# Eight experts fed from one sorted gather instead of one gather each, and their scatter moved to the turn between two experts

## The chip, the core and the metric

One core of a Trainium2 chip runs the whole kernel as one program. The metric is the device time in microseconds (us) of one execution. The core has five engines with their own instruction streams: PE (TensorE, matmuls), DVE (VectorE), ACT (ScalarE), POOL (GpSimd) and SP (SyncE, which here only issues DMAs). They meet at semaphores. SBUF holds tiles of 128 partitions; PE writes into eight PSUM banks of 128 x 512 float32.

## The reference

Two layers of a decoder trunk over 256 tokens of width 1024. Each has a token mixer and then a feed-forward part: a dense SwiGLU in layer 0, and in layer 1 eight SwiGLU experts of hidden width 3584, of which each token uses the best two. What matters here is the second:

```
def _moe(h, router_w, router_b, wg, wu, wd):
    logits = (h @ router_w + router_b).astype(jnp.float32)
    top_v, top_i = lax.top_k(logits, MOE_TOPK)
    top_w = jax.nn.softmax(top_v, axis=-1)
    gates = jnp.sum(top_w[..., None] * jax.nn.one_hot(top_i, N_EXPERTS, dtype=jnp.float32), axis=-2)
    out = jnp.zeros_like(h)
    for e in range(N_EXPERTS):
        out = out + gates[..., e:e + 1] * _swiglu(h, wg[e], wu[e], wd[e])
    return out
```

The result is added to x through a per-channel gate, and a last RMSNorm follows. 256 tokens with two picks each make 512 (token, expert) pairs, spread unevenly over the experts.

## The kernel before

Everything is float32. About half of the time goes to the mixers and the dense part, which the change leaves alone. The expert part begins with the router, at 1033 us, and runs to the end.

**Weights.** An expert is 42 units of 1 MB: seven groups `g`, each with two gate units, two up units and two down units. SP streams them through 14 slots (L485); a slot is loaded again when PE has used its unit, so SP follows PE by at most 14 units. The first 14 units of the first expert are loaded before the router is done.

**Router (L1740 to L1776).** DVE picks the two best experts of each token as masks. PE turns the masks into running counts, five products of 8 columns each (L941 to L945). A token's count within an expert, less one, is its key. DVE compares the keys with a row of slot numbers, `slot_f`, and this gives `p_m`, the gather matrix of one expert (L1774). Expert 0 comes first and the other seven follow in an order worked out on the chip from their counts, by turns a crowded and a light one; `ranks`, `places`, `counts`, `turns`, `gates`, `keys` and `expert_gates` are small steps of DVE for this, put between the copies of the first gather.

**Gather (L955, L981).** For each expert, eight column blocks m: two products (two token tiles) of `h_tm` with `p_m` into one of the banks 6 and 7, then a DVE copy to `xg` (L1835, L1854). It writes 256 slots where the expert has over 128 tokens, else 128. It stands between two experts in the program of PE (the block `tail` of `expert_loop`), and the next expert's first product waits for the copies.

**Expert body.** There are six variants by the rounded token count n: 32 (`quarter_rows`), 64, 96, 128 (`rows_stationary`), 160 and 256 (`weights_stationary`). Its sums for the output lie in banks 2 to 5, and ACT takes them out to `ysb` at the end (L1440, L1275).

**Scatter (L966 to L978).** The output of expert e is put back to its tokens while expert e+1 runs: after groups 1 to 4 of the next expert, one step each, into banks 6 and 7, where DVE adds it to `xT` (L1846). Each step waits for the merges of the step before. At the end of the last expert the four steps stand alone. The scatter matrix `pgT` is made in two moves: DVE compares keys, times gates, into `pg_m` (`matrices`), and before the last down product PE transposes it (`prepare`, L1185) and DVE copies it (L1949). In the first expert the scatter steps run on a zero matrix.

The branches on counts (`by_rows`, `by_size`, the compare chain of L450 and L453) are executed by each engine's own sequencer.

Of the kernel before, what the change touches and what calls it, by code (L numbers as in the profile page):

```python
# [17 lines left out]
P = 128  # L18
# [75 lines left out]
def trunk(nc, x_cols, c_cols, par_cols, ada_units, dense_units, moe_units, out):  # L94
# [7 lines left out]
    with ctx:  # L102
# [30 lines left out]
        stk = sb("stk", [P, QUARTER])  # L133
        modc = sb("modc", [P, 48])
# [7 lines left out]
        key9 = sb("key9", [P, TT, EXPERTS + 1])  # L142
        gate9 = sb("gate9", [P, TT, EXPERTS + 1])
# [28 lines left out]
        xg = proj[:, 16:24, :]  # L172
        h_tm = proj[:, 24:32, :].rearrange("p (t a) n -> p t (a n)", t=TT)
        p_m = proj[:, 32:34, :]
        pg_m = proj[:, 34:36, :]
        pgT = proj[:, 36:38, :]
        silx = proj[:, 38:42, :].rearrange("p (b j) n -> p b (j n)", b=2)
        hst = proj[:, 42:46, :].rearrange("p (b j) n -> p b (j n)", b=2)
        o_tm = proj[:, 24:32, :].rearrange("p (t a) n -> p t (a n)", t=TT)
# [34 lines left out]
        order_c = swap[:, 192:256].rearrange("p (a b) -> p a b", a=8)  # L214
        gr = xc[:, 0:6, :].rearrange("p (a b) n -> p a b n", a=3)
# [104 lines left out]
        p_s = sem("gather_matrix")  # L320
        pg_s = sem("scatter_matrix")
# [99 lines left out]
        def expert_loop(eng, expert, between=None):  # L421
# [13 lines left out]
            if between is not None:  # L435
                with nc.body(tail, valid_engines=own):
# [8 lines left out]
                    between(following, coming)  # L445
                    eng.br(head)
            with nc.body(head, valid_engines=own):
                e = nc.snap(index, engines=own, min_val=0, max_val=EXPERTS - 1)
                count, before = on(now), on(past)
                to_form[SIZES[-1]] = eng.br_cond(count > SIZES[-2], f"{tag}_{SIZES[-1]}", f"{tag}_over_{SIZES[-3]}")  # L450
# [6 lines left out]
            for n in SIZES:  # L457
                with nc.body(f"{tag}_{n}", valid_engines=own):
                    ahead = eng.mark_branch_hint_location()
                    after = expert(n, e, before)  # L460
# [129 lines left out]
        def _(pe):  # L590
# [350 lines left out]
            mm(ps[:, 1, 0:8], striu[:, :], mask[:, 0, :], start=True, stop=True)  # L941
            mm(ps[:, 1, 8:16], ones[:, :], mask[:, 0, :], start=True, stop=False)
            mm(ps[:, 1, 8:16], striu[:, :], mask[:, 1, :], start=False, stop=True)
            mm(ps[:, 1, 16:24], ones[:, :], mask[:, 0, :], start=True, stop=False)
            mm(ps[:, 1, 16:24], ones[:, :], mask[:, 1, :], start=False, stop=True).then_inc(cum_s, 1)  # L945

            C_BASE, PER = KT, 1 + 2 * KT

            def gather(free_at, n):  # L950

                for m in range(KT):
                    pe.wait_ge(cf_s, free_at + m)
                    for t in range(TT):
                        last = mm(ps[:, 6 + (m + 1) % 2, 0:n], h_tm[:, t, m * P:(m + 1) * P], p_m[:, t, 0:n],  # L955
                                  start=(t == 0), stop=(t == TT - 1))
                    last.then_inc(c_s, 1)

            pe.wait_ge(htm_s, TT)
            pe.wait_ge(p_s, 1)  # L960
            gather(CF0 + C_BASE - 1, SEQ)
            pe.wait_ge(rk_s, 2)
            C1 = C_BASE + KT

            def scatter(n, step, free_at):

                pe.wait_ge(cf_s, free_at + 2 * step)
                for c in range(2):
                    m = step + 4 * c
                    if n == HALF:  # L970
                        r0 = HALF * c
                        mm(ps[:, 6 + c, 0:SEQ], ysb[r0:r0 + HALF, 0, step * P:(step + 1) * P], pgT[r0:r0 + HALF, 0, :],
                           start=True, stop=True).then_inc(c_s, 1)
                        continue
                    for st in range(n // P):
                        last = mm(ps[:, 6 + c, 0:SEQ], ysb[:, st, m * P:(m + 1) * P], pgT[:, st, :],
                                  start=(st == 0), stop=(st == n // P - 1))
                    last.then_inc(c_s, 1)  # L978

            def gather_next(following, count):  # L980
                pe.wait_ge(p_s, following + 1)  # L981
                with pe.If(count <= P):
                    gather(following * PER + CF0 + C1 + KT - PER, P)
                with pe.Else():
                    gather(following * PER + CF0 + C1 + KT - PER, SEQ)

            def expert(n, e, before):
# [7 lines left out]

                def tokens_ready(kind, g, h):
                    if kind == "g" and g == 0:
                        pe.wait_ge(cf_s, e * PER + CF0 + C1 - 4 * (1 - h))

                def rows_stationary(n):  # L1000
# [67 lines left out]
                def quarter_rows(n):  # L1068
# [44 lines left out]
                    for g in range(1, GE):  # L1113
                        gate(g)
                        sum_and_turn(g - 1)
# [3 lines left out]
                        if 1 <= g <= 4:  # L1119
                            scatter_before(g - 1)  # L1120
                        down_quarter(g - 1)
                    sum_and_turn(GE - 1)
                    prepare(n)
# [4 lines left out]
                def weights_stationary(n):  # L1128
# [30 lines left out]
                    for g in range(GE):  # L1159
# [4 lines left out]
                        if 1 <= g <= 4:  # L1164
                            scatter_before(g - 1)
                        if g:
                            down_wide(g - 1)
                    prepare(n)
# [3 lines left out]

                def scatter_before(step):

# [22 lines left out]
            def scatter_last(rows):  # L1197
                for step in range(4):
                    scatter(rows, step, PER * EXPERTS + CF0 + C1 - KT)

# [856 lines left out]
```

## Time and profile before

| | |
|---|---|
| median of three runs | 2001.78 us (2000.38 to 2004.81) |
| the profiled execution | 2002.5 us, its span 2000.6 us |
| PE busy | 1872.0 us (94%) |
| DVE, ACT, POOL busy | 509.1, 279.6, 351.7 us |
| DMA | 533.87 MB, mean 267 GB/s |
| expert part, first product to the end of the last down product | 1055.5 to 1973.6 us |

The experts in their order, from PE's timeline:

| place | n | first product | last product ends |
|---|---|---|---|
| 0 | 32 | 1055.5 | 1133.2 |
| 1 | 160 | 1140.3 | 1330.6 |
| 2 | 32 | 1336.3 | 1411.9 |
| 3 | 128 | 1419.1 | 1571.0 |
| 4 | 32 | 1575.9 | 1652.5 |
| 5 | 96 | 1658.5 | 1783.6 |
| 6 | 64 | 1791.0 | 1872.7 |
| 7 | 64 | 1877.9 | 1973.6 |

PE's busy share of 94% says little by itself: where PE waits for weights, a shorter program of PE ends no earlier. So the views by stretch and the timeline of PE are what to read: which stretch ends with a wait for DMA, and which doesn't.

### The profile page before, as it was taken

The numbers are of one execution on the slowest core, as the hardware profiler recorded it, in microseconds if no ns is written. First come the engines' busy times: TensorE is split into PE (matmuls) and PEld (weight loads), VectorE is DVE, ScalarE is ACT, GpSimd is POOL, SyncE is SP. The second block draws the span as 40 slices with busy tenths as digits, with TensorE's granted clock in tenths as the row PEclk, the third lists the DMA queues.
The fourth block names the chain that finished last, engine by engine and source line by source line (L and its number), as shares of the span: only waits on it lengthen the run. The fifth ranks groups of instructions, "written<-read, shape, count | busy, mean of one in ns | idle before, by whom it ended". The sixth has DMA issues, their size and how long they took to land.

```text
span 2000.6 us, 27713 instructions
## 1 busy us (share of the span) xinstructions
PE 1872.0 (94%) x11005; PEld 1313.5 (66%) x11006; DVE 509.1 (25%) x1131; ACT 279.6 (14%) x517; POOL 351.7 (18%) x215
## 2 busy tenths in 40 slices
PE   7999799989999899999978899998999989999986
PEld 5888588877777688888863587753444436555543
DVE  1794734110000285333332100011100110101111
ACT  2204212010000311423021000010000100010002
POOL 2709910059996000000000000000000000000000
PEclk8999899999999999999989899998999989999998
DMA  9645533157765344333458976669998899999994
GB/s 388 252 152 209 194 127 119 64 227 263 269 250 189 147 148 147 126 106 106 168 231 354 420 319 253 253 265 421 420 389 293 329 421 419 420 371 422 422 422 180
DMA packets 73845, 533.87 MB, mean 267 GB/s; under 512 B 8320, under 2 KB 8320, under 8 KB 8960
## 3 DMA queue, kind: packets, MB, share of 16 engines
q1 hardware_dynamic: 67680, 489.72, 62.2%
q0 software_dynamic: 5760, 41.95, 5.7%
q8 instruction: 92, 1.51, 0.3%
q10 hardware_dynamic: 288, 0.50, 0.1%
q14 instruction: 25, 0.20, 0.0%
HBM read 531.08 MB, written 1.05 MB: 266 GB/s over the span
## 4 chain that ended last, share of the span: by engine, by line
PE 81%; DMA 7%; SPq 4%; DVE 4%; ACT 2%; issue 2%; POOL 1%; ACTq 0%; DVEq 0%
PE ps L657 21%; PE ps L1012 12%; PE ps L720 8%; PE ps L729 7%; PE ps L1139 6%; PE ps L1047 6%; SPq L485 4%; PE ps L740 4%; PE ps L1155 3%; DMA ring<-in_moe_units 3%; PE ps L1075 3%; PE ps L955 2%; DMA sq<-in_moe_units 1%; DMA xc<-in_moe_units 1%; PE ps L1105 1%
## 5 line engine op out<-in xcount | busy, mean ns | idle before, releaser
L657 PE MATMUL ps<-hT,ring 128*128 128x256 f32 x2048 | 454.3, 383 | 5.0 <-ACT hT L1262 5.0
L657 PEld LDWEIGHTS ps<-hT,ring 128*128 128x128 f32 x2048 | 389.8, 192 | 61.9 <-issue 8.3
L576 POOL TENSOR_TENSOR aring<-aring,ccol 128x2048 f32<-128x2048 f32 x40 | 145.0, 3625 | 236.3 <-ACT hT L1262 162.6
L729 PE MATMUL ps<-hT,ring 128*128 128x256 f32 x704 | 156.7, 384 | 4.0 <-ACT hT L1262 4.0
L582 POOL TENSOR_TENSOR aring<-aring 128x1024 f32<-128x1024 f32 x80 | 149.5, 1869 | 6.3
L729 PEld LDWEIGHTS ps<-hT,ring 128*128 128x128 f32 x704 | 135.0, 193 | 22.8 <-issue 4.4
L1012 PE MATMUL ps<-ring,proj 128*64 128x256 f32 (+2 forms) x1144 | 131.6, 362 | 3.6 <-DMA ring<-in_moe_units 3.6
L1886 DVE TENSOR_TENSOR proj<-proj,ps 128x256 f32<-128x256 f32 (+2 forms) x28 | 14.6, 521 | 379.8 <-PE ps L1012 379.8
L1012 PEld LDWEIGHTS ps<-ring,proj 128*64 128x64 f32 (+2 forms) x1144 | 74.8, 132 | 55.3 <-issue 33.0
L1616 DVE SCALAR_TENSOR_TENSOR misc<-cpad,par,misc 128x256 f32<-128x256 f32 x240 | 102.7, 505 | 0.0
L1267 ACT ACTIVATE proj<-ps 128x512 f32<-128x512 f32 x64 | 38.2, 596 | 328.8 <-PE ps L657 328.8
L720 PE MATMUL ps<-proj,ring 128*128 128x256 f32 x384 | 83.4, 379 | 0.0
L720 PEld LDWEIGHTS ps<-proj,ring 128*128 128x128 f32 x384 | 72.8, 190 | 9.9
L740 PE MATMUL ps<-ring,proj 128*128 128x512 f32 x176 | 77.3, 592 | 0.0
L1385 ACT ACTIVATE proj<-ps 128x256 f32<-128x256 f32 (+2 forms) x28 | 13.0, 464 | 381.4 <-PE ps L1012 381.4
L1729 DVE TENSOR_TENSOR proj<-proj,ps 128x256 f32<-128x256 f32 x22 | 9.3, 421 | 210.8 <-ACT proj L1365 210.8
L1139 PE MATMUL ps<-proj,ring 128*128 128x160 f32 x416 | 60.0, 300 | 0.0
L720 PE MATMUL ps<-hT,ring 128*128 128x256 f32 x256 | 55.8, 380 | 3.0 <-DVE hT L1693 3.0
L1139 PEld LDWEIGHTS ps<-proj,ring 128*128 128x128 f32 x416 | 57.5, 190 | 0.8 <-issue 0.8
L740 PEld LDWEIGHTS ps<-ring,proj 128*128 128x128 f32 x176 | 33.4, 190 | 37.3 <-issue 36.8
L1094 PEld LDWEIGHTS ps<-stk,proj 128*128 128x128 f32 x336 | 44.3, 212 | 20.1 <-issue 20.1
L720 PEld LDWEIGHTS ps<-hT,ring 128*128 128x128 f32 x256 | 48.5, 190 | 10.3 <-DVE hT L1693 3.8
(347 smaller groups left out, 2086.2 us busy)
## 6 DMA issues: line engine op xcount, KB each, us to landing
ring<-in_moe_units SPq DMA_DIRECT2D x144, 1024.0 KB, 17.0
ring<-in_dense_units SPq DMA_DIRECT2D x121, 1024.0 KB, 5.0
aring<-in_moe_units SPq DMA_DIRECT2D x48, 1024.0 KB, 17.3
proj<-in_moe_units SPq DMA_DIRECT2D x48, 1024.0 KB, 18.7
aring<-in_ada_units POOLq DMA_DIRECT2D x40, 1024.0 KB, 6.2
extra<-in_moe_units SPq DMA_DIRECT2D x24, 1024.0 KB, 16.6
xc<-in_moe_units SPq DMA_DIRECT2D x24, 1024.0 KB, 20.6
misc<-in_moe_units SPq DMA_DIRECT2D x24, 1024.0 KB, 19.7
```

The costliest lines, as they stand in the source:

```text
L485: sp.dma_start(eslot[u % EXP_SLOTS], moe_units[ds(expert, 1), u].rearrange("e p n -> p (e n)")).then_inc(efull[u % EXP_SLOTS], 16)
L576: last = g.tensor_tensor(w, w, ccol[:, :].unsqueeze(2).broadcast_to([P, KT, 256]), ALU.mult)
L582: last = g.tensor_tensor(dst, w[:, 0:half_k, :], w[:, half_k:2 * half_k, :], ALU.add)
L657: last = mm(ps[:, n % 2, j * SEQ:(j + 1) * SEQ], wide(s)[:, k, j * P:(j + 1) * P], hT[:, k, :], start=(k == 0), stop=(k == KT - 1))
L720: last = mm(ps[:, idx % 2, j * SEQ:(j + 1) * SEQ], view(s)[:, k, (cols + j) * P:(cols + j + 1) * P], rhs[:, k, :], start=(k == 0), stop=(k ...
L729: last = mm(ps[:, j, c0:c0 + n], wide(w)[:, k, j * P:(j + 1) * P], x_src[:, k, 0:n], start=(k == 0), stop=(k == KT - 1))
L740: last = mm(dst, hm[:, b, j, t * P:t * P + rows], rows2(slot)[:, j, hf * 512:(hf + 1) * 512], start=(first and j == 0), stop=(stop and j = ...
L1012: last = mm(ps[rows * c:rows * (c + 1), bank, 4 * t0:4 * (t0 + rows)], xg[:, 4 * h + k, t0:t0 + rows], w[:, k, 4 * rows * c:4 * rows * (c ...
L1047: last = mm(dst, hmt[:, g % 2, h0:h0 + rows], w[:, i, cols], start=(g == 0 and j == 0), stop=(g == GE - 1 and j == 3))
L1075: last = mm(ps[n * k:n * (k + 1), bank, :], xg[:, 4 * h + k, 0:n], w[:, k, :], start=(h == 0), stop=(h == 1))
L1139: last = mm(ps[:, j % 2, c0:c0 + n], w[:, k, j * P:(j + 1) * P], xg[:, 4 * h + k, 0:n], start=(h == 0 and k == 0), stop=(h == 1 and k == 3))
L1616: v.scalar_tensor_tensor(cacc[:, m, :], cpad[:, m, ds(k, SEQ)], cwcol[:, l, ds(k * CT + m, 1)], cacc[:, m, :], ALU.mult, ALU.add).then_inc ...
```

## The change

It replaces eight gathers by one, builds the scatter matrix another way, and moves the scatter.

1. **Gather.** Five running sums become eleven products of 8 columns: a token's slot now counts all pairs of lower experts too, so the 512 pairs have 512 sorted slots. `p_all` (two tiles of 128 x 512) holds both picks. One gather of eight column blocks by 512 columns fills `xg_all`; ACT copies the first 256 columns to `xg` for expert 0. For each later expert DVE copies its window of columns from `xg_all` to `xg`, 64, 128 or 256 wide, from a start read from `first_slot`, once its own work for the expert before is done.
2. **Scatter matrix.** PE spreads each token's slot numbers and gates along rows (eight products of 128 columns, after the gather); ACT takes them to `slot_rows` and `gate_rows`. In group 2 of an expert DVE compares `slot_rows` with the slot number of each row (`slot_of_row`) and multiplies by `gate_rows`. That is `pgT` itself: the transposes of `prepare` and their copy go.
3. **Scatter.** It moves out of the next expert's groups to the block between the experts, all four steps in one go, into the four banks 4 to 7. PE waits there for `pgT`, for the merges before, and for ACT's copy of the output (`ye_s`). The next expert's first product stands behind it in PE's queue. The dummy scatter in the first expert goes. The merges of DVE run after the scatter, while the next expert starts.

```
@@ PE, router
-            mm(ps[:, 1, 0:8], striu[:, :], mask[:, 0, :], start=True, stop=True)
...
+            lower = [(ones, below[:, t, :]) for t in range(TT)]
+            token_sums(0, lower + [(striu, mask[:, 0, :])])
+            token_sums(8, lower + [(ones, mask[:, 0, :]), (striu, mask[:, 1, :])])
+            token_sums(16, lower)
+            token_sums(24, [(ones, mask[:, t, :]) for t in range(TT)]).then_inc(cum_s, 1)
@@ PE, gather
-            gather(CF0 + C_BASE - 1, SEQ)
+            for m in range(KT):
+                if m >= 2:
+                    pe.wait_ge(cf_s, CF0 + KT + m - 1)
+                for t in range(TT):
+                    pe.wait_ge(p_s, t + 1)
+                    last = mm(ps[:, 6 + m % 2, :], h_tm[:, t, m * P:(m + 1) * P], p_all[:, t, :],
+                              start=(t == 0), stop=(t == TT - 1))
+                last.then_inc(c_s, 1)
+            for values, bank in ((token_slot, 3), (token_gate, 2)):
+                if bank == 2:
+                    pe.wait_ge(gate1_s, 1)
+                for pick in range(2):
                     for t in range(TT):
+                        c0 = (TT * pick + t) * P
+                        last = mm(ps[:, bank, c0:c0 + P], values[:, pick, t:t + 1].broadcast_to([P, P]), ident[:, :],
+                                  start=True, stop=True)
+                last.then_inc(row_s, 1)
@@ PE, between two experts (before: gather_next)
+            def scatter(n):
+                for step in range(4):
+                    for c in range(2):
+                        m = step + 4 * c
+                        dst = ps[:, 4 + 2 * (step // 2) + c, (step % 2) * SEQ:(step % 2 + 1) * SEQ]
...
+            def scatter_done(following, coming, done):
+                pe.wait_ge(pg_s, 2 * following)
+                pe.wait_ge(cf_s, following * PER + CF0 + C1 - PER)
+                pe.wait_ge(ye_s, following + 1)
+                by_rows(pe, done, scatter)
@@ PE, in each variant of the expert body
                         gate(g)
+                        if g == 1:
+                            banks_merged()
                         h_transpose(g - 1)
                         up(g)
-                        if 1 <= g <= 4:
-                            scatter_before(g - 1)
                         down_rows(g - 1)
                     h_transpose(GE - 1)
-                    prepare(n)
                     down_rows(GE - 1)
@@ ACT, before the experts
+            for m in range(KT):
+                act.wait_ge(cf_s, CF0 + KT + m + 1)
+                a_(xg[:, m, :], xg_all[:, m, 0:SEQ], ACT.Copy).then_inc(xg_s, 1)
+            for i, (rows, bank) in enumerate(((slot_rows, 3), (gate_rows, 2))):
+                act.wait_ge(row_s, i + 1)
+                a_(rows, ps[:, bank, :].rearrange("p (a b) -> p a b", a=2), ACT.Copy).then_inc(rows_s, 1)
@@ DVE, router
-            for t in range(TT):
-                last = v.tensor_scalar(p_m[:, t, :], slot_f[:, :], key9[:, t, 0:1], None, ALU.is_equal)
+            for t in range(TT):
+                last = v.tensor_scalar(p_all[:, t, :], slots, token_slot[:, 0, t:t + 1], None, ALU.is_equal)
+            then_wait(last)
+            for t in range(TT):
+                v.scalar_tensor_tensor(p_all[:, t, :], slots, token_slot[:, 1, t:t + 1], p_all[:, t, :],
+                                       ALU.is_equal, ALU.add).then_inc(p_s, 1)
...
-                v.tensor_copy(xg[:, m, :], ps[:, 6 + (m + 1) % 2, 0:SEQ]).then_inc(cf_s, 1)
+                v.tensor_copy(xg_all[:, m, 0:2 * SEQ], ps[:, 6 + m % 2, :]).then_inc(cf_s, 1)
@@ DVE, between two experts
+            def merged_next(following, coming, done):
                 def tokens(width):
+                    first = dve.value_load(first_slot[0:1, ds(following, 1)], min_val=0, max_val=5 * P - width)
+                    v.tensor_copy(xg[:, :, 0:width], xg_all[:, :, ds(first, width)]).then_inc(xg_s, KT)
+                by_rows(dve, coming, tokens)
+                for step in range(4):
+                    merge(step, following * PER + (C1 - PER))
@@ DVE, group 2 of an expert (before: matrices)
+                def matrix():
...
+                        v.scalar_tensor_tensor(picks, slot_rows, slot_of_row[:, kind + st, ds(e, 1)], gate_rows,
+                                               ALU.is_equal, ALU.mult).then_inc(pk_s, 1)
+                        v.tensor_tensor(pgT[:, st, :], picks[:, 0, :], picks[:, 1, :], ALU.add).then_inc(pg_s, 1)
```

## Rows read from the trace of the kernel before

**Rows 1.** Stretches: PE, PEld, DVE, ACT, POOL busy (count), granted clock, DMA share, GB/s

```profile
1150.00:1300.00 150.00, 150.00 (x997) 120.22 (x996) 11.71 (x35) 6.99 (x23) 0.00 (x0) 1.00 0.70 276
1345.00:1380.00 35.00, 33.05 (x252) 15.87 (x248) 8.54 (x19) 2.62 (x6) 0.00 (x0) 1.00 1.01 422
1780.00:1795.00 15.00, 12.04 (x110) 7.74 (x104) 2.34 (x8) 4.23 (x8) 0.00 (x0) 1.00 0.72 269
```

**Rows 2.** Chain of waits, router: start, us on the chain, what

```profile
1040.95 0.43 PE ps L942 x2
1042.66 1.56 issue
```

**Rows 3.** Timeline, router to first product: start, us, engine, line, what, count, [idle before]

```profile
1043.51 0.62 DVE L1774 TENSOR_SCALAR proj<-slot_f,key 128x256 f32<-128x256 f32 x2
1044.23 8.26 PE L955 MATMUL ps<-proj 128*128 128x256 f32 x28 [1.56 <-issue]
1055.53 1.92 PE L1075 MATMUL ps<-aring,proj 128*32 128x512 f32 x16 [1.42 <-DVE proj L1835]
```

**Rows 4.** Stretch at the start of the first gather

```profile
1044.00:1046.00 2.00, 1.77 (x4) 1.51 (x5) 0.61 (x2) 1.03 (x1) 0.00 (x0) 0.50 0.03 12
```

**Rows 5.** Timeline of PE: eight products of 512 columns in expert 3

```profile
1426.06 3.60 PE L1012 MATMUL ps<-extra,proj 128*128 128x512 f32 x8
```

**Rows 6.** Timeline of PE: last and first products around each turn between experts

```profile
1131.35 1.87 PE L1105 MATMUL ps<-sq,proj 128*32 128x512 f32 x8
1140.26 2.44 PE L1139 MATMUL ps<-proj,aring 128*128 128x160 f32 x16
...
1325.89 4.70 PE L1155 MATMUL ps<-sq,proj 128*128 128x512 f32 x24
1336.28 1.92 PE L1075 MATMUL ps<-aring,proj 128*32 128x512 f32 x16 [0.76 <-DVE proj L1854]
...
1410.83 1.04 PE L1105 MATMUL ps<-sq,proj 128*32 128x512 f32 x8
1419.09 7.13 PE L1012 MATMUL ps<-aring,proj 128*128 128x512 f32 x16 [1.43 <-issue]
...
1567.38 3.60 PE L1047 MATMUL ps<-sq,proj 128*128 128x512 f32 x8
1575.92 1.92 PE L1075 MATMUL ps<-aring,proj 128*32 128x512 f32 x16 [0.76 <-DVE proj L1854]
...
1651.13 1.40 PE L1105 MATMUL ps<-sq,proj 128*32 128x512 f32 x8
1652.83 4.44 PE L955 MATMUL ps<-proj 128*128 128x128 f32 x32 [0.29 <-issue]
1658.50 4.47 PE L1012 MATMUL ps<-aring,proj 128*64 128x256 f32 x56 [1.23 <-DVE proj L1854]
...
1780.68 2.94 PE L1047 MATMUL ps<-sq,proj 128*64 128x512 f32 x24
1791.02 3.67 PE L1012 MATMUL ps<-aring,proj 128*64 128x256 f32 x32 [1.74 <-issue]
```

**Rows 7.** Timeline of ACT: the output taken out, n = 160 and 64

```profile
1330.65 2.50 ACT L1275 ACTIVATE proj<-ps 128x512 f32<-128x512 f32 x6 [18.37 <-PE ps L1155]
1973.61 0.60 ACT L1440 ACTIVATE proj<-ps 128x512 f32<-128x512 f32 x1 [4.15 <-PE ps L1047]
```

**Rows 8.** Timeline of PE: one scatter step, for 32 or 64, 96 or 128, and 160 rows

```profile
1202.71 0.70 PE L972 MATMUL ps<-proj 64*128 64x256 f32 x4
...
1345.32 1.99 PE L976 MATMUL ps<-proj 128*128 128x256 f32 x8
...
1584.96 1.13 PE L976 MATMUL ps<-proj 128*128 128x256 f32 x4
```

**Rows 9.** Timeline of PE: the last scatter and the sums of the last norm

```profile
1976.68 1.23 PE L972 MATMUL ps<-proj 64*128 64x256 f32 x4 [3.12 <-issue]
...
1984.39 4.68 PE L635 MATMUL ps<-sq,ones 128*128 128x256 f32 x16
```

More of the change, by code:

```diff
@@ L448, in expert_loop @@
                 e = nc.snap(index, engines=own, min_val=0, max_val=EXPERTS - 1)
-                count, before = on(now), on(past)
+                count = on(now)
                 to_form[SIZES[-1]] = eng.br_cond(count > SIZES[-2], f"{tag}_{SIZES[-1]}", f"{tag}_over_{SIZES[-3]}")
@@ L459, in expert_loop @@
                     ahead = eng.mark_branch_hint_location()
-                    after = expert(n, e, before)
+                    after = expert(n, e)
                     nc.regs_mov(past, count)
@@ L962, in _ @@
[L962 to L987, printed above, removed]
+            below = rt[:, 13, :, :]
+            def token_sums(c0, terms):
+                for i, (weights, values) in enumerate(terms):
+                    last = mm(ps[:, 1, c0:c0 + EXPERTS], weights[:, :], values, start=(i == 0), stop=(i == len(terms) - 1))
+                return last
@@ L1171, in weights_stationary @@
                     return after
-                def scatter_before(step):
-                    pe.wait_ge(ye_s, e + 1)
-                    by_rows(pe, before, lambda rows: scatter(rows, step, e * PER + CF0 + C1))
-                def prepare(n):
-                    slot_tiles = (n + P - 1) // P
-                    pe.wait_ge(pg_s, e + 1)
-                    pe.wait_ge(cf_s, e * PER + CF0 + C1 + KT)
-                    for st in range(slot_tiles):
-                        for t in range(TT):
-                            last = nc.tensor.transpose(ps[:, 6, st * SEQ + t * P:st * SEQ + (t + 1) * P],
-                                                       pg_m[:, t, st * P:(st + 1) * P], ident[:, :])
-                    last.then_inc(c_s, 1)
                 if n == QUARTER:
@@ L1191, in expert @@
                 return rows_stationary(n) if n <= P else weights_stationary(n)
-            expert_loop(pe, expert, gather_next)
+            expert_loop(pe, expert, scatter_done)
             last_count = pe.value_load(cnt[0:1, EXPERTS:EXPERTS + 1], min_val=0, max_val=SEQ)
-            pe.wait_ge(ye_s, EXPERTS + 1)
-            def scatter_last(rows):
-                for step in range(4):
-                    scatter(rows, step, PER * EXPERTS + CF0 + C1 - KT)
-            by_rows(pe, last_count, scatter_last)
+            scatter_done(EXPERTS, None, last_count)
             norm_sums(2 * DEPTH)
@@ L1745, in _ @@
             narrow_copy(DEPTH)
+            v.memset(xg_all[:, :, 2 * SEQ:], 0.0)
+            v.tensor_copy(slots[:, 0:SEQ], slot_f[:, :])
+            v.tensor_scalar(slots[:, SEQ:2 * SEQ], slot_f[:, :], float(SEQ), None, ALU.add)
             dve.wait_ge(lg_s, 1)
```

205 lines of the change are left out of this document (101 added, 104 removed).

## The prediction

> **What bounds the kernel now.** I read the stretches first, then PE's timeline around each turn between two experts, then the chain of waits in the router. The change touches nothing before the router, so only the time from 1040 us on is in play.
>
> The stretches show two kinds of expert [rows 1]. In place 1 (n = 160) PE is busy all the time at full clock and the DMA engines at a share of 0.70: PE bounds, and each microsecond off its program counts. In place 2 (n = 32) DMA is full and PE has gaps: the weights bound. By the same reading places 0, 2, 4 and 7 are of the second kind, places 1, 3 and 5 of the first. The third stretch is the turn from place 5 to 6: DMA is idle for 28% of 15 us, 4.2 us, because all 14 slots are full and SP waits for PE to use a unit. After that turn places 6 and 7 need 70 more units, and the stream is full to the end, so the end of place 7 is set by when place 6 begins.
>
> From this follows how a saving is passed on. In a weight-bound expert the stream restarts when the expert's first units are used, because before the turn the slots are full. An edit inside it is worth nothing, an edit that moves its first product moves its end by as much. In a PE-bound expert both count. In places 6 and 7 nothing inside counts, the turn between them neither. What counts is therefore: the router up to the first product of place 0; the six turns 0 to 1 up to 5 to 6; the program of places 1, 3 and 5; and what follows the last down product.
>
> **Router.** The running sums take 0.43 us a product on the chain [rows 2]. Eleven instead of five: +2.6. Three small compares more for the masks, without waits, 0.3 (0 to 0.6). From the last sum to the gather's first product it was 1.56 us [rows 2], in which two compares of 256 columns took 0.62 [rows 3]. Now: two small steps (0.4), two compares of 512 columns (1.24, twice the row), one compare-and-add of 512 (0.75 by the same row, 0.6 to 1.0) and a semaphore, 2.5: +0.9. Together +3.8.
>
> From the gather's first product to the first expert product it was 11.3 us [rows 3]: the gather waited for copies. The new gather has 8 x 2 products, in float32 two passes each, 32 instructions of 512 columns. One costs 0.43 to 0.45 at full clock [rows 5], so 13.8 us. DVE has 1.7 us for each block, and its copy and small step need about 1.4, so PE sets the pace. The granted clock was 0.50 at the start of the gather, which is 1.2 GHz [rows 4]; PE had been nearly idle before it. I keep about 3.5 us at the half clock, +1.7 (0 to 2.5). Then come the eight row products, 16 instructions of 128 columns; 32 such take 4.44 [rows 6], so 2.2. They stand ahead of expert 0 in PE's program and nothing hides them; ACT's copies to `xg` are done meanwhile. Last the count is loaded and the compare chain run: 1.42 before [rows 3], and I take 1.7 as the sequencer can hardly do it sooner. Sum 19.4, so +8.1. The router costs **+11.9** (8.5 to 16).
>
> **The six turns.** The time between the end of the last down product and the next expert's first product was [rows 6]: 7.0, 5.7, 7.2, 4.9, 6.0 and 7.4 us, mostly gather. The new turn has four parts. (a) ACT takes the output out: 0.6 for n = 32 or 64, 2.5 for n = 160 [rows 7]; n = 96 needs six copies too, n = 128 two, 1.1; plus 0.1 to start. (b) After this wait the sequencer branches on the count and issues. No row shows a branch behind a wait inside the loop. From below: the old gather began 0.29 after the last product [rows 6]. From above: the last scatter began 3.12 after it [rows 9], 2.4 of it after ACT's copy. I take 0.4, since the turns inside the loop run the same block as the old gather while the last scatter first leaves the loop. (c) Four scatter steps. A step costs 0.63 to 0.70 for up to 64 rows, 1.06 for 96 or 128, 1.93 for 160 [rows 8]: 2.5, 4.25 or 7.7. (d) The jump into the next expert. It left PE idle for 0.76 to 1.74 [rows 6]. A long scatter hides it. Behind a short one I put 0.5, 2.5 and 1.3 at turns 0, 2 and 4, more where the old row says "issue" with 1.43.
>
> New turns: 4.1, 10.7, 6.1, 5.9, 4.9, 7.3. Differences: -2.9, +5.0, -1.1, +1.0, -1.1, -0.1, together +0.8. The second is the telling one: the scatter of 160 rows costs nothing today, in the middle of weight-bound place 2, and 7.7 us in the open afterwards. Two turns idle PE for about 3 us, and after a gap of 3.12 the last scatter ran at half rate (1.23 for a step that takes 0.70 otherwise [rows 8, 9]), so +1.3. Turns: **+2.1** (-3 to +14).
>
> Queued behind PE's new wait for ACT is the whole next expert, and behind that SP, which loads only as units are used. DVE's copy of the window to `xg` lies beside the last down products and the merges beside the next expert's first products: 0.
>
> **Inside places 1, 3 and 5.** Four scatter steps go from each, 12 at 0.70 [rows 8]: -8.4. `prepare` goes too. In places 3 and 5 its transposes lie in a wait for ACT, 0; in place 1 four of them at 0.14 are on the path, -0.5. The new comparison of rows on DVE is hidden, DVE being busy for 12 of 150 us there [rows 1]. **-8.9** (-9.5 to -8).
>
> **The end.** Today the four last steps wait for merges in turn, and from the first step to the end of the norm's sums it is 12.4 us [rows 9]. With four banks: 4 x 1.18 plus 4.68, 9.4. **-3.0** (-4.5 to -2).
>
> **Sum.** +11.9 +2.1 -8.9 -3.0 = +2.1. On the profiled execution's 2002.5 that is 2004.6; this execution lies 0.7 above the median, so **2003.9** for the median. A measurement of this kernel can tell about 0.2% (4.0 us) from no change: faster means below 1997.8, slower above 2005.8.
>
> **Rivals.**
>
> (1) *Faster: the clock and the jumps.* If PE has risen to full clock before the gather (the longer sums keep it busier) 1.7 goes; if the gaps at the turns don't drop it, 1.3; if the jumps are hidden behind short scatters too, 3; and a shorter start of place 0, 0.6. Together -6.6: 1997.3. For it: 2.4 and 1.3 are small gaps next to the 7 us that preceded the half clock in the router. Against: the clock was down after 3.12 us at the end [rows 9]. It decides from about 6.1 us of such gains. Chance 0.18.
>
> (2) *Slower: the branch behind the wait.* Each turn pays 2.4 after ACT's copy [rows 7, 9] instead of 0.4, six times 2.0: 2015.9. Against: the old tail has branches too and starts its gather within 0.29 at best [rows 6]. Chance 0.12. The Trainium skill speaks for this rival and so against this change: "Runtime: NRT & Kernel Launch", section "Instruction fetch mechanics", says that prefetch is sequential, and that a taken branch to a target outside the pages at hand stalls until a DMA has fetched it. The new block between experts is longer than the old one, and its branch comes after a wait. By that rule the sum would be this rival's; by the 0.29 us the forecast's.
>
> (3) *Slower: the gather follows its copies.* The copy to `xg_all` is twice as wide, and DVE's small steps lie between; if a block takes 2.2 us instead of 1.7, +4: 2007.9. Chance 0.12.
>
> (4) *The saving inside the experts is not there.* Between places 4 and 6 I save 4.0 us, and DMA has 4.2 of idle time to give [rows 1]; if it has less, because units of 2.5 us come in at the wrong moment, or if a crowded expert begins before its first four units are there, 1 to 2 us are lost: 2005.4. Chance 0.08.
>
> **Numbers.** The forecast itself has 0.50, with 1999.5 to 2008.5 as its own range. Of it 0.33 is within 0.2%, 0.13 slower, 0.04 faster. Rival 1 gives 0.10 faster, 0.08 same; rival 2 0.12 slower; rival 3 0.10 slower, 0.02 same; rival 4 0.03 slower, 0.05 same. Faster 0.14, same 0.48, slower 0.38. The range runs from 1997.5 to 2011.5; it leaves rival 2 out and the far half of rival 1.
>
> **What the profile after would show.** First product of place 0 near 1067.4. Six turns of the lengths above, that of the 160-row scatter near 11 us with 7.7 of PE work. Places 1, 3 and 5 shorter by 3.3, 2.8 and 2.8 from first to last product; places 0, 2 and 4 as long as before, with more idle time of PE. Two pairs of merges after the last scatter and no wait between its steps. The prediction fails if the gather's blocks lie more than 1.9 us apart, if scatters begin more than 1 us after ACT's copy, or if places 0, 2 and 4 change their length by more than 1.5 us: then the weight stream is not what I think.

## The result

Before and after ran four times each. Every kernel of an experiment below has its ratio to the kernel before as it ran on the same chip in the same session.

| | median (lowest to highest) us | profiled execution: time, span | granted clock |
|---|---|---|---|
| before | 2001.08 (1999.86 to 2004.81) | 2002.5, 2000.6 | 0.967 |
| after | 2016.18 (2014.7 to 2017.57) | 2014.96, 2013.2 | 0.955 |

The ratio is 1.0069, 95% interval 1.0055 to 1.0083: 0.69% slower. The forecast was 2003.9 with a range of 1997.5 to 2011.5, so both missed. The time is that of rival 2 (2015.9). Whether its mechanism is the cause as well is the first question.

The page of after (engines' busy us, share of the span, instructions; then shares of the chain that ended last):

```profile
PE 1861.8 (92%) x10775; PEld 1302.4 (65%) x10776; DVE 492.8 (24%) x1066; ACT 283.7 (14%) x527; POOL 351.3 (17%) x215
PE 78%; DMA 8%; SPq 6%; DVE 3%; issue 2%; ACT 2%; POOL 1%; ACTq 0%; DVEq 0%
```

The router, in PE's timeline of after (start, us, line, what, count, [idle before]; compare rows 2 and 3):

```profile
1038.23 0.61 PE L958 MATMUL ps<-heads,ones 128*128 128x8 f32 x4 [1.66 <-DVE heads L1780]
...
1044.16 16.80 PE L976 MATMUL ps<-proj 128*128 128x512 f32 x32 [2.30 <-DVE proj L1793]
1060.79 1.05 PE L985 MATMUL ps<-ident,token_slot 128*128 128x128 f32 x8
1061.68 1.06 PE L985 MATMUL ps<-ident,token_gate 128*128 128x128 f32 x8
1062.67 1.92 PE L1102 MATMUL ps<-aring,hT 128*32 128x512 f32 x15
```

Its clock at the start of the gather (start:end, length, busy times, granted clock, DMA share, GB/s):

```profile
1044.00:1048.00 4.00, 3.84 (x5) 1.81 (x6) 1.09 (x7) 0.00 (x0) 0.00 (x0) 0.50 0.00 0
1048.00:1052.00 4.00, 4.00 (x8) 1.67 (x8) 2.22 (x8) 0.83 (x2) 0.00 (x0) 0.77 0.00 0
```

The gather's 32 instructions take 16.8 us, those of the first 4 us at the half clock, and no wait for a copy splits the row. The first expert product stands at 1062.67 instead of 1055.53. The work ahead of the router, which the change doesn't touch, ran 2.4 us ahead of that in the trace of before. So the change costs 9.5 here.

The turns of after, from the same view (compare rows 6 and 8; a turn is the stretch between two experts, and turn 0 stands behind place 0):

```profile
1140.06 2.00 PE L998 MATMUL ps<-proj 64*128 64x256 f32 x16 [1.67 <-ACT proj L1449]
1146.41 4.63 PE L1165 MATMUL ps<-hT,aring 128*128 128x160 f32 x16 [4.36 <-issue]
...
1339.02 8.86 PE L1002 MATMUL ps<-proj 128*128 128x256 f32 x32 [3.14 <-ACT proj L1277]
1347.81 1.07 PE L1102 MATMUL ps<-aring,hT 128*32 128x512 f32 x8
...
1426.41 2.00 PE L998 MATMUL ps<-proj 64*128 64x256 f32 x16 [0.86 <-ACT proj L1449]
1432.93 10.12 PE L1040 MATMUL ps<-aring,hT 128*128 128x512 f32 x16 [4.52 <-issue]
```

Two things are to be seen. The scatter follows ACT's copy closely: at turn 2 it begins 0.86 us after the last product, and 0.6 of that is the copy (at turn 0 it is 1.67). But behind a short scatter PE stands for 4.4 and 4.5 us on "issue" before the next expert's first product, where the forecast had 0.5 and 2.5. And the next expert's first 16 instructions then take 4.63 and 10.12 us, which took 2.44 and 7.13 before [rows 6]: the half clock follows the gap. The stretch behind turn 0 says the same (columns as above):

```profile
1146.00:1150.00 4.00, 3.59 (x13) 3.60 (x14) 0.00 (x0) 0.00 (x0) 0.00 (x0) 0.50 1.02 418
1150.00:1154.00 4.00, 4.00 (x23) 4.00 (x23) 0.00 (x0) 0.09 (x1) 0.00 (x0) 0.72 1.00 416
```

The end (compare rows 9) has one wait, then all steps, then the sums. From the last down product's end (1991.08) to the end of the sums it takes 10.5 us instead of 15.5.

```profile
1994.28 2.79 PE L998 MATMUL ps<-proj 64*128 64x256 f32 x16 [3.20 <-issue]
1997.07 4.54 PE L648 MATMUL ps<-sq,ones 128*128 128x256 f32 x16
```

The same reading of PE's timeline gives this table. Besides before and after it has five kernels of the experiments below. A place's length goes from its first product to the end of its last down product, a turn from there to the next first product (us). The last column is the stretch from the first product of place 6 to the end of place 7.

| kernel | first product | places 0 to 5 | turns 0 to 5 | 6 and 7 |
|---|---|---|---|---|
| before | 1055.5 | 77.7 190.3 75.6 151.9 76.6 125.1 | 7.0 5.7 7.2 4.9 6.0 7.4 | 182.6 |
| after | 1062.7 | 75.7 189.5 77.7 151.6 79.6 122.9 | 8.0 11.9 7.4 5.2 7.5 8.6 | 182.8 |
| code shifted (r_align) | 1062.2 | 78.2 188.3 77.7 148.6 75.6 122.9 | 5.4 11.9 5.0 5.2 6.9 8.6 | 182.6 |
| before, shifted badly (r_cross) | 1054.3 | 80.3 192.9 79.6 153.7 75.7 126.5 | 13.4 5.7 10.1 4.9 11.3 8.4 | 182.3 |
| filled turn (r_late) | 1065.5 | 79.8 186.5 79.6 148.5 75.5 121.3 | 18.8 24.1 16.7 19.0 17.0 20.7 | 182.0 |
| early hints (r_inline2) | 1063.8 | 78.0 187.1 77.3 148.6 76.9 122.0 | 2.7 9.8 2.7 4.9 4.5 9.4 | 182.3 |
| and scatter in groups (r_groups2) | 1061.9 | 77.4 192.8 76.4 151.9 79.2 124.5 | 1.2 0.9 1.5 0 0 0.7 | 191.1 |

### The profile page after: what moved, and what is told of

Read it like the earlier page. It is cut to its first block, busy times and chain, and to the rows that moved or that the text cites. A ratio compares the mean times of both kernels' runs of the same rounds, so it can differ in the third digit from the quotient of the medians.

```text
span 2013.2 us, 26982 instructions
## 1 busy us (share of the span) xinstructions
PE 1861.8 (92%) x10775; PEld 1302.4 (65%) x10776; DVE 492.8 (24%) x1066; ACT 283.7 (14%) x527; POOL 351.3 (17%) x215
## 4 chain that ended last, share of the span: by engine, by line
PE 78%; DMA 8%; SPq 6%; DVE 3%; issue 2%; ACT 2%; POOL 1%; ACTq 0%; DVEq 0%
PE ps L670 21%; PE ps L1040 11%; PE ps L733 8%; PE ps L742 7%; PE ps L1165 6%; SPq L498 6%; PE ps L1075 5%; PE ps L753 4%; PE ps L1181 3%; DMA sq<-in_moe_units 3%; PE ps L1102 2%; DMA ring<-in_moe_units 1%; DMA xc<-in_moe_units 1%; DMA misc<-in_ada_units 1%; PE ps L1121 1%
## 5 line engine op out<-in xcount | busy, mean ns | idle before, releaser
L670 PEld LDWEIGHTS ps<-hT,ring 128*128 128x128 f32 x2048 | 390.7, 192 | 62.2 <-issue 8.3
L742 PEld LDWEIGHTS ps<-hT,ring 128*128 128x128 f32 x704 | 136.6, 195 | 23.5 <-issue 4.4
L595 POOL TENSOR_TENSOR aring<-aring 128x1024 f32<-128x1024 f32 x80 | 148.5, 1857 | 6.3
L1040 PE MATMUL ps<-ring,hT 128*64 128x256 f32 (+2 forms) x1144 | 132.3, 362 | 5.4 <-DMA ring<-in_moe_units 5.4
L1040 PEld LDWEIGHTS ps<-ring,hT 128*64 128x64 f32 (+2 forms) x1144 | 75.4, 132 | 57.2 <-issue 34.3
L733 PEld LDWEIGHTS ps<-proj,ring 128*128 128x128 f32 x384 | 72.8, 190 | 9.9
L753 PE MATMUL ps<-ring,proj 128*128 128x512 f32 x176 | 77.3, 592 | 0.0
L1121 PEld LDWEIGHTS ps<-stk,proj 128*128 128x128 f32 x336 | 48.6, 230 | 21.9 <-issue 21.9
L1165 PE MATMUL ps<-hT,ring 128*128 128x160 f32 x416 | 60.0, 300 | 0.0
L1165 PEld LDWEIGHTS ps<-hT,ring 128*128 128x128 f32 x416 | 57.5, 190 | 0.8 <-issue 0.8
L1102 PE MATMUL ps<-ring,hT 128*32 128x512 f32 x312 | 46.0, 692 | 10.9 <-DMA ring<-in_moe_units 10.9
## 6 DMA issues: line engine op xcount, KB each, us to landing
ring<-in_moe_units SPq DMA_DIRECT2D x144, 1024.0 KB, 15.6
proj<-in_moe_units SPq DMA_DIRECT2D x48, 1024.0 KB, 18.8
extra<-in_moe_units SPq DMA_DIRECT2D x24, 1024.0 KB, 15.4
```

The lines of the kernel that those rows point to most:

```text
L595: last = g.tensor_tensor(dst, w[:, 0:half_k, :], w[:, half_k:2 * half_k, :], ALU.add)
L670: last = mm(ps[:, n % 2, j * SEQ:(j + 1) * SEQ], wide(s)[:, k, j * P:(j + 1) * P], hT[:, k, :], start=(k == 0), stop=(k == KT - 1))
L733: last = mm(ps[:, idx % 2, j * SEQ:(j + 1) * SEQ], view(s)[:, k, (cols + j) * P:(cols + j + 1) * P], rhs[:, k, :], start=(k == 0), stop=(k ...
L742: last = mm(ps[:, j, c0:c0 + n], wide(w)[:, k, j * P:(j + 1) * P], x_src[:, k, 0:n], start=(k == 0), stop=(k == KT - 1))
L753: last = mm(dst, hm[:, b, j, t * P:t * P + rows], rows2(slot)[:, j, hf * 512:(hf + 1) * 512], start=(first and j == 0), stop=(stop and j = ...
L1040: last = mm(ps[rows * c:rows * (c + 1), bank, 4 * t0:4 * (t0 + rows)], xg[:, 4 * h + k, t0:t0 + rows], w[:, k, 4 * rows * c:4 * rows * (c ...
```

## The experiments

**What the leap waits for.** A form is the code for one rounded token count. First thing in the tail, the block between two experts, PE's program gives a hint which form comes next (`mark_branch_hint_location`). Behind the tail's work it branches there; this far branch is the leap. The trace has records of PE's sequencer and of the DMA packets that bring its code. One such packet has 16384 bytes, a piece of code; in the compiled program that is 256 instructions of 64 bytes. Read from these records, in us:

```
turn  kernel  hint     far branch, took  code packet      hint to branch's end
 0    before  1131.90  1139.42  0.43     1135.7           7.9
 2    before  1412.40  1417.63  1.13     1416.2           6.4
 4    before  1652.00  1657.35  0.74     1655.6           6.1
 0    after   1139.19  1140.73  5.33     1143.6           6.9
 2    after   1424.09  1427.23  5.28     1430.0           8.4
 4    after   1667.07  1671.15  5.30     1674.0           9.4
```

The first kernel shifts the code of after:

```diff
+            if unused is not None:            # in expert_loop, ahead of the tail
+                with nc.body(f"{tag}_unused", valid_engines=own):
+                    unused()                  # 45 matmuls, reached by no execution
+                    eng.br(end)
```

> The changed kernel with 45 matmuls added that are never executed: they stand in TensorE's program ahead of the end-of-expert code and shift its addresses, so that the scatter, the hint and the far branch of an expert's end lie in one 16 KB piece of code instead of across two. Nothing that runs is changed. Theory A (fetching the next piece of code while the scatter runs throws away what the hint has fetched, and the leap into the next expert waits for a whole fetch): after turns 0, 2 and 4 the idle time ahead of the next expert's first instruction falls from 4.4, 4.5 and 2.9 us by 2 to 3.5 each, turn 5's scatter ends sooner, and the half-clock products after it go; 2004 to 2008 us. Theory B (the hint comes too shortly ahead of the branch, 1.5 to 4.1 us, or the branch overtakes it; where the code lies is of no account): no change, 2015 to 2017 us.

Measured: 2003.95 us, ratio to before 1.0007 (0.9997 to 1.0016). Nothing that is executed differs from after, and 12.2 us of median are gone (12.4 by the two ratios). Its turns 0 and 2:

```profile
1141.25 2.00 PE L1002 MATMUL ps<-proj 64*128 64x256 f32 x16 [0.86 <-ACT proj L1457]
1145.79 3.47 PE L1169 MATMUL ps<-hT,aring 128*128 128x160 f32 x16 [2.54 <-issue]
...
1424.57 2.00 PE L1002 MATMUL ps<-proj 64*128 64x256 f32 x16 [0.86 <-ACT proj L1457]
1428.75 7.13 PE L1044 MATMUL ps<-aring,hT 128*128 128x512 f32 x16 [2.19 <-issue]
```

The idle time is 2.5 and 2.2 instead of 4.4 and 4.5, and behind the shorter gap at turn 2 the first products run at full clock (granted 1.00, and 7.13 us). The place of the code was the cause of most of it, then, but not of the whole: the far branches of turns 0, 2 and 4 still take 3.6, 3.2 and 4.5 us. They end 6.4, 6.2 and 6.3 us after the hint, as at turns 2 and 4 of before. So with an undisturbed fetch the target is ready about 6.3 us after the hint, and the scatter of up to 64 rows leaves only 1.8 to 3.1 us between hint and branch (theory B's part).

The second kernel does the same harm to the kernel before. 13 such matmuls shift its tail across the same boundary:

> The kernel before with 13 matmuls added that are never executed, which shift the code of the gather between two experts so that it lies across two 16 KB pieces of TensorE's program. Nothing that runs is changed. Theory A (fetching the next piece throws away what the hint has fetched): the leap into the next expert, 0.4 to 1.2 us before, takes some 5 us at turns 0, 2, 4 and 5; with the clock's loss behind it 8 to 16 us more, 2009 to 2017. Theory B (only hint to branch time counts, which stays at 5 us and more here): no change, 2000 to 2003 us.

Measured: 2026.99 us, ratio 1.0115 (1.0098 to 1.0131), more than either theory said.

```profile
1134.54 8.04 PE L959 MATMUL ps<-proj 128*128 128x256 f32 x32
1148.04 4.63 PE L1143 MATMUL ps<-proj,aring 128*128 128x160 f32 x16 [5.47 <-issue]
...
1436.46 3.78 PE L1016 MATMUL ps<-aring,proj 128*128 128x512 f32 x4 [5.66 <-issue]
```

The far branches of turns 0, 2 and 4 take 6.1, 5.2 and 5.4 us. The six turns grow by 15.6 us in sum and the places 0 to 5 by 11.5 (table), partly at the half clock behind the gaps; why place 2, which follows no long gap, is 4.0 longer I can't say. Theory A's direction stands in both kernels. B is refuted as the sole cause, since here the hint comes 5.3 us and more ahead of the far branch. The packets come 12.3, 9.2 and 8.1 us after the hint, with none in between. So no fetched code was thrown away, as the expectation had it: the fetch started late.

The third fills the turn of after:

```diff
                 by_rows(pe, done, scatter)
+                if coming is not None:
+                    for _ in range(32):
+                        mm(ps[:, 0, 0:SEQ], ident[:, :], pgT[:, 0, :], start=True, stop=True)
```

> The changed kernel with 32 matmuls of 256 columns (about 3.4 us at full clock) executed behind the scatter of each of the six turns inside the loop, ahead of the branch into the next expert; their result is used by nobody. Theory B (the branch comes too soon behind the hint): the leap at turns 0, 2 and 4 falls from 5.3 to about 1 us, so those turns get some 1 us shorter each, and the turns 1, 3 and 5 3.4 longer: about +7, 2021 to 2025 us. Theory A (the hint is thrown away by the fetch of the next piece of code, and the tail still lies across two): the leap stays 5.3 us and all six turns get 3.4 longer: about +18 to +21 us, 2033 to 2037.

Measured: 2082.1 us, ratio 1.0391 (1.0368 to 1.0414). I had mis-sized the filling by four: a float32 product makes two instructions of 0.22 us each, so the filling takes 14 us a turn and the time says nothing about either theory. The trace does.

```profile
1149.87 14.39 PE L1013 MATMUL ps<-proj,ident 128*128 128x256 f32 x64
1164.09 2.20 PE L1168 MATMUL ps<-hT,aring 128*128 128x160 f32 x15
```

The leap is free (the branch takes 0.34), although the tail still lies across two pieces. So the hint isn't lost: it is held back. Its packet starts 6.1, 6.4 and 4.6 us after the hint, and each time 3.5 to 3.7 after the branch that leaves the scatter over the boundary (1146.23, 1455.20, 1715.17). The far branch comes only 9 to 11 us after the packet, so it can't have asked for it. In after, the same distance holds: the branch over the boundary stands at 1140.12, 1426.48 and 1670.27, and the packets come 3.5, 3.6 and 3.7 later. There, and at turns 2 and 4 of the second kernel, the packet also comes 2.7 to 2.9 us after the far branch, so these turns alone could not tell a held hint from a fetch that the branch began. Turn 0 of the second kernel, where the gather's last products cross the boundary without a branch, is the odd one: about 4 us from the crossing, 3.6 from the far branch.

The mechanism that fits these turns is an inference from their times: the fetch of the hinted piece starts only when TensorE's sequencer has left the first of the two pieces, and about 6 us from there on the target is ready. The Trainium skill ("Runtime: NRT & Kernel Launch", section "Instruction fetch mechanics") says that a sequencer holds two lines of 16 KiB, fetched in order, and that a taken branch outside them stalls for a DMA fetch. The traces agree: such a branch took 5.2 to 6.1 us here. With two lines, a third piece has to wait until one is left, as the held packets do. The same section also gives PE 128 KiB, more than two lines; the traces fit two.

**Taking the leap out.** In the next kernel PE's loop has no shared tail. Each form's own code ends with its scatter, whose size is known there, so the branch on the row count goes; the chain of compares follows. The hint is given earlier, ahead of the last two down products. Unused matmuls place the code so that no boundary comes late between hint and leap.

```diff
+                        if g == GE - 1:
+                            hint(after)          # ahead of the last two down products
                         down_rows(g - 1)
...
-            expert_loop(pe, expert, scatter_done)
+            scatter_loop(pe, expert, scatter_after, {32: 21, 96: 34, 128: 22})
```

> The changed kernel with TensorE's expert loop rearranged: the scatter of each form stands at the end of that form's own code (no shared tail, no branch on the row count), the hint for the next expert's form is given before the last two down products (9 us or so ahead of the leap instead of 1.5 to 4), and unused matmuls place the stretch from hint to leap within one 16 KB piece of code, or let the boundary come soon after the hint. Same products and scatters in the same order. Theory A (a leap is free when its code has been fetched, and the fetch is complete some 6.2 us after the hint, as in the shifted kernel): leaps of 0.3 to 1 us in all turns, so 8 to 9 us less at the turns than the shifted kernel, and one or two more from the clock: 1992 to 1997 us, faster than before. Rival (the leap costs its 3 to 4.5 us whatever the lead, or TensorE's gap is needed by another engine): 2002 to 2005 us.

Measured: 2004.08 us, ratio 1.0012 (1.0003 to 1.0022), which looks like the expectation's rival. Its trace shows something else, my own slip: the unused matmuls ahead of one form were executed once, behind the last expert.

```profile
1972.20 2.00 PE L1052 MATMUL ps<-proj 64*128 64x256 f32 x16 [0.79 <-ACT proj L1507]
1974.13 11.83 PE L465 MATMUL ps<-heads,ones 128*128 128x8 f32 x68
1985.89 1.65 PE L702 MATMUL ps<-sq,ones 128*128 128x256 f32 x3
```

With them truly out of the way:

> The kernel with early hints and scatters at the turn again, with the 34 unused matmuls now where they are never executed (in its first form they ran once behind the last expert and took 11.8 us of TensorE, seen in its trace). Nothing else changes. Theory A: 2004.1 less 11.8, or 1991 to 1994 us. Rival (the matmuls were hidden by the merges and squares that the norm sums wait for): 1997 to 2004.

Measured: 1993.86 us, ratio 0.9953 (0.994 to 0.9966): theory A.

```profile
1142.58 2.00 PE L1052 MATMUL ps<-proj 64*128 64x256 f32 x16 [0.81 <-ACT proj L1507]
1144.51 2.44 PE L1223 MATMUL ps<-hT,aring 128*128 128x160 f32 x16
```

No idle time stands ahead of the next expert and its first products take 2.44, as before. The turns 0 to 5 now sum to 34.0 us (after 48.6, before 38.2). The scatter begins 0.81 after the last down product, with no branch behind the wait for ACT. With that branch it was 0.86 (first kernel). So the branch, rival 2's mechanism, costs 0.05.

**Where the scatter belongs.** The same loop, but with part three of the change undone: the scatter is done in four steps of two banks within groups 1 to 4 of the next expert, each merged there.

```diff
+                        if 1 <= g <= 4:
+                            scatter_before(g - 1)
                         down_rows(g - 1)
...
-                    scatter_after(n, e)
```

> The same loop with early hints, but the third part of the change is undone: each expert's scatter is again done in four steps of two banks inside the groups 1 to 4 of the next expert (merged there by VectorE), the last one behind the loop; the gather into sorted slots and the new scatter matrix stay. Theory P (the scatter costs TensorE what it takes wherever it stands, and the last one in four banks saves the 5 us found at the end): about 3 to 8 us slower than the early-hint loop with scatters at the turn, 1996 to 2004 us. Rival (at the turn the scatter is dearer, because it waits for ScalarE's copy and idles TensorE into the slow clock, while inside the groups it has no wait): 3 to 8 us faster than that loop, below 1992 us.

Measured: 1994.11 us, ratio 0.9958 (0.9944 to 0.9972). That lies between the two theories, and level with the early-hint kernel. But this kernel has the old end, 15.4 us behind the last down product, so its loop is the faster one. With the last scatter in four banks, in the code right behind the last expert:

> The kernel with early hints and the scatters inside the groups of the next expert, and now with the last scatter in four banks, standing in the code right behind the last expert so that no leap stands ahead of it. In the groups' first form the last down product's end to the norm sums' end took 15.4 us. Theory (that stretch falls to the 10.5 us of the changed kernel or a little less, and nothing else moves): 1994.1 less 5, 1987 to 1990 us. Rival (places 6 and 7 are paced by the weights' stream, which ends when it ends, so that the four banks save only what lies behind it): the same saving, since the stretch lies behind the stream; but if the scatter's squares or the sums wait for VectorE anyway, 1991 to 1994.

Measured: 1985.42 us, ratio 0.9911 (0.9897 to 0.9925), a little better than either theory. The last scatter no longer stands behind the leap out of the loop: from the last down product to the end of the sums it takes 8.2 us.

```profile
1140.56 4.44 PE L1222 MATMUL ps<-hT,aring 128*128 128x160 f32 x16 [1.25 <-DVE hT L1957]
...
1960.29 2.00 PE L1272 MATMUL ps<-proj 64*128 64x256 f32 x16 [0.79 <-ACT proj L1528]
1964.00 3.72 PE L704 MATMUL ps<-sq,ones 128*128 128x256 f32 x16 [1.71 <-ACT sq L1311]
```

Against the early-hint kernel this is 0.42% less (0.9953 against 0.9911), 8.4 us of median. Both have early hints and the last scatter in four banks. The end accounts for 2.2 of it (8.2 us against 10.4, in which PE stands for 1.7 on "issue" in the middle of the sums). The other 6 or so are the scatter's place. So the scatter at the turn is a loss of its own in this change, beside the leap. The table says how: the turns fall by 29.7 us more. Of that 12.3 come back in the places 0 to 5 (5.7, 3.3, 2.3 and 2.5 in places 1, 3, 4 and 5, while 0 and 2 get 1.5 shorter) and 8.8 in places 6 and 7, which the weight stream sets. Of the 5.7 in place 1, 2.0 are the clock's (4.44 against 2.44): although only 1.25 us of idle time stand ahead of it, the granted clock was 0.50 already at the end of place 0. The weight stream in numbers:

```profile
1868.50:1970.10 101.60, 83.65 (x576) 40.74 (x574) 6.51 (x16) 5.33 (x14) 0.00 (x0) 1.00 0.98 406
```

```profile
1760.00:1775.00 15.00, 13.65 (x129) 6.90 (x123) 0.00 (x0) 4.83 (x9) 0.00 (x0) 1.00 1.02 420
1640.00:1960.00 320.00, 296.04 (x2913) 156.59 (x2905) 25.26 (x54) 25.58 (x54) 0.00 (x0) 1.00 0.99 412
...
1855.80:1959.50 103.70, 86.69 (x590) 41.95 (x590) 7.54 (x17) 6.70 (x16) 0.00 (x0) 1.00 0.96 397
```

The first fence is place 7 of the early-hint kernel (its columns are those of rows 1). The second is of the kernel with scatters in groups: the stretch around the turn to place 6, the places 5 to 7, and place 7. Across that turn the stream now runs at 1.02, where it stood still for 28% before [rows 1]. So there is no slack left for it to catch up, and 6 and 7 take 191.1 us instead of 182.3. What turn 5 saves is taken back behind it: from the first product of place 5 to the end of place 7 it is 316.3 us here, 313.7 in the early-hint kernel and 314.3 in after. From place 5 to the end of place 7 the DMA engines' share is 0.99: that stretch is bound by the stream.

**The end alone.** The kernel before with only its last scatter in four banks:

```diff
-                for step in range(4):
-                    scatter(rows, step, PER * EXPERTS + CF0 + C1 - KT)
+                pe.wait_ge(cf_s, PER * EXPERTS + CF0 + C1 - KT)
+                for step in range(4):
+                    for c in range(2):
+                        dst = ps[:, 4 + 2 * (step // 2) + c, (step % 2) * SEQ:(step % 2 + 1) * SEQ]
...
```

> The kernel before with one part of the change alone: the scatter behind the last expert goes into four banks at once instead of four steps of two banks; everything inside the loop stays. The prediction's term was 3.0 us, the changed kernel's trace shows 5.0. Theory M (the 5.0 is this part): 1996 to 1998 us. Rival P (3.0 is this part, and 2 us of the 5.0 came with the other parts): 1998.5 to 2000.

Measured: 1997.85 us, ratio 0.9966 (0.9954 to 0.9979), 6.4 us of median.

```profile
1977.99 2.00 PE L1205 MATMUL ps<-proj 64*128 64x256 f32 x16 [2.75 <-issue]
1980.78 3.72 PE L635 MATMUL ps<-sq,ones 128*128 128x256 f32 x16 [0.79 <-ACT sq L1242]
```

From the last down product's end (1975.24) to the end of the sums it is 9.3 us instead of 15.5. That is theory M, and a little more.

## Why the prediction was wrong

The sum, on the profiled executions' spans (+12.6 us; the work ahead of the router gave 2.4 back, which is not the change's):

| term | forecast | measured | |
|---|---|---|---|
| router | +11.9 | +9.5 | inside its range (8.5 to 16); the gather has the pace of PE, as said |
| six turns | +2.1 | +10.4 | the miss |
| places 1, 3, 5 | -8.9 | -3.4 (-0.8, -0.3, -2.2) | the miss's other half |
| places 0, 2, 4 | 0 | +3.1 (-2.0, +2.1, +3.0) | |
| end | -3.0 | -5.0 | mis-sized |

**The turns, part (d).** Parts (a) and (b) held: after the last down product the scatters began at 1.7, 3.1, 0.9, 1.6, 0.9 and 3.3 us, forecast 1.1 to 3.0. Part (c) held in the main: they took 2.0, 8.9, 2.0, 3.7, 3.8 and 5.4, together 2.1 over the forecast, and where they were longer than forecast (turns 1, 4 and 5) the granted clock was 0.50 to 0.66 at their start. The jump was put at 0.5, 2.5 and 1.3 for turns 0, 2 and 4, read from the idle time in rows 6; it took 4.4, 4.5 and 2.9 of idle. That is 7.5 of the 8.3 us missed. The step that failed is taking the jump's old idle time as its price. That idle time was the rest of a 6.3 us fetch that the gather had covered. The change shortens the cover, and it moves the code so that the fetch starts later still. I did not ask what work hid the fetch and what it would cost without it. Shifting the code alone gave back 12.2 of the 15.1 us between the medians, and the shifted kernel ran at 2003.95. That this is the forecast's number to the tenth is chance: its turns are 2.7 us longer and its end 2.0 us shorter than forecast, and its first product comes 5.2 us sooner.

**Places 1, 3 and 5.** The mechanism was right. Without the gaps ahead of them they are shorter by 3.2, 3.3 and 3.1 us (early hints), forecast 3.3, 2.8 and 2.8. In after, the first products of places 1 and 3 ran at the half clock and lost 2.2 and 3.0 us (4.63 against 2.44, 10.12 against 7.13). The forecast's clock term, +1.3 in all, was too small because the gaps were.

**The end.** -3.0 took the steps at 1.18 us and the sums at 4.68, both at the rate they had behind an idle stretch [rows 9]. In after the steps took 2.79 together and the sums 4.54. The kernel with this part alone gains 6.2 there: at a granted clock of 1.00 its four steps take 2.0 us, 0.50 each back to back, and its sums 3.72. The term was mis-sized, by the clock again and by taking the price of a step that stands alone.

**Rivals.** Rival 2 (0.12) named the time, 2015.9, but a wrong cause: that it came out so near is luck. Inside the loop the scatters began 0.2 to 1.0 us after ACT's copy, not 2.4, and the branch itself costs 0.05. The 2.4 of rows 9 was the rest of the leap out of the loop, a far branch of 3.8 us that ends at 1975.8. The rule of the Trainium skill quoted there was the right one. I had hung it on the branch into the scatter, which is near, instead of the leap into the next form, which is far. Rival 3 did not occur. Of rival 1, jumps hidden behind short scatters came about only in the early-hint kernel. Of rival 4: places 6 and 7 took 182.8 against 182.6, the stream's pace as forecast, and 182.0 even when 16.8 us of turn stood between them.

**Fails if.** Places 0, 2 and 4 were to keep their length within 1.5 us, and none did. Place 2 takes 77.3 to 79.6 us instead of 75.6 in every kernel of the table with a scatter at the turn ahead of it, with DMA at 0.98; why, stays open. The gather's blocks lay 3.6 and 2.8 us apart at first, over the 1.9 of the prediction, but by the low clock; from the third on they lay 1.72 apart. Of the scatters only that of turn 0 began as much as 1.0 us after ACT's copy. So of the three signs of being wrong only that of the places was a real one.

## What to carry to other kernels

Idle time ahead of a far branch is what is left of a code fetch after its cover; before a block between hint and branch is shortened, the time that a fetch takes from the hint (about 6.3 us here) has to be set against what will remain of the block, and the hint given earlier. A size or time that changes for no visible reason after an edit can be the code's place: shift it by instructions that never run and time both. Work moved from the inside of a stage into the turn between stages is paid in full there, while turns that are emptied are paid back in part where the weight stream bounds.

## What the runs showed of the hardware

- A far branch whose target was fetched took 0.34 to 0.36 us (filled turn). One whose target wasn't took 5.2 to 6.1 us (after and the kernel before, shifted badly), with 415 to 419 GB/s moving beside it. Within one 16384-byte piece of code, and where the branch had to wait, the target was ready 6.1 to 6.4 us after the hint at turns 2 and 4 of before and turns 0, 2 and 4 of the shifted kernel, and 6.8 and 7.1 after it at turn 5 of the two.
- Where a boundary between two pieces lay between hint and far branch, the packet came 3.5 to 3.7 us after the branch over the boundary, in eight turns of three kernels, and not 3.6 to 3.9 after the hint. Thirteen never executed matmuls made the kernel before 1.15% slower.
- After a gap of 4.4 us PE's granted clock was 0.50 for the next 4 us (1.2 GHz). After a gap of 2.2 us, at turn 2 of the shifted kernel, it was 1.00 (2.4 GHz) for the first products.
